# The last product of a feed-forward layer by seven block products instead of eight

## The chip, the cores and the metric

The kernel runs on one core of a Trainium2 chip. Its time is the device time of one execution in microseconds; the time before is the median of 3 executions. A profile of one further execution gives the span from the first to the last instruction, and the work of TensorE (PE; its weight loads are PEld), VectorE (DVE), ScalarE (ACT), GpSimd (POOL) and the DMA queues. SyncE (SP) only issues transfers.

## The reference

256 tokens of 1024 channels in float32 pass through two blocks: an mLSTM and a gated linear attention layer, each with a mixture of 16 experts behind it, and then an attention layer with a gated feed-forward layer. The change is in the very last part:

```python
def conv_ffn(y, w_up, conv_w, conv_b, w_down):
    u = y @ w_up
    ...
    gate, val = jnp.split(u, 2, axis=-1)
    return (jax.nn.silu(gate) * val) @ w_down
...
        y = rms_norm_2(h, ffn_norm[i])
        h = h + conv_ffn(y, w_up[i], conv_w[i], conv_b[i], w_down[i])
    return rms_norm_2(h, final_norm)
```

The last product is (256 tokens x 2816) @ (2816 x 1024). The result is added to the stream h, and each token is divided by its root mean square and multiplied by a gain row.

## The kernel before

All engines have instruction lists of their own, written out by hand, and meet by semaphores. Weights come through `weight_ring`, 9 slots of 128 x 4096 float32 in SBUF, in one order that SyncE's list fixes; a slot is loaded again when TensorE has counted `tile_used` for its last content, and `landed[slot]` tells TensorE of the arrival (`arrived`).

The feed-forward is `ffn()` of each engine. There are UPT = 11 tiles of w_up and N_DOWN = 6 tiles of w_down (numbers T_UP and T_DOWN on); a tile of w_down holds four blocks of 128 rows by 1024 columns, the last one two. FB = 22 such blocks are the 2816 rows.

- Up (L1172, in `up`): for each tile, 32 matmuls of a 128 x 128 block of weights on the 256 turned tokens `xT`, into banks 0 to 5 by turns. ScalarE takes the banks with the middle tap of the convolution (L1499, `taps`), VectorE adds the two other taps (L1966, `convolve`), ScalarE applies SiLU (L1508), and VectorE multiplies gate and value (L1977) into `ffh`, 22 blocks of 128 channels x 256 tokens in `phase_room`; each of the 11 multiplications makes two blocks and counts `ff_ready`.
- Down (L1206): for each tile of w_down, for both halves `tt` of the tokens, for its blocks `k` and both halves `j` of the 1024 columns, one matmul with 128 tokens of `ffh` as the stationary operand and 512 columns of the tile as the moving one:

```python
mm(PS[4 + 2 * tt + j][:, :], ffh[:, k, tt * P:(tt + 1) * P],
   w[:, k - 4 * i, j * 512:(j + 1) * 512], start=(k == 0), stop=(k == FB - 1))
```

  So 22 x 2 x 2 = 88 matmuls go to four banks (4 to 7), one for each quarter of the output. The last tile is ordered so that the quarters end one after the other (`out_rows`, `last_half`, `tile_used`).
- The end, `final_norm` on VectorE: `add` (L1985) adds a bank to a quarter of the stream `x_tok`; ScalarE squares it and sums along the row (L1515); `total` (L1990) adds the two halves' sums; ScalarE takes the root (L1523, `final_deviation`); VectorE takes the reciprocal (L2005, L2012) and `scale` (L1995) writes the finished quarter to `acc`, from where SyncE sends it out (L544). Of the three waiting steps the scale of the first quarter runs while ScalarE squares the last one.

Of the kernel before, what the change touches and what calls it, by code (L numbers as in the profile page):

```python
# [17 lines left out]
ALU = mybir.AluOpType  # L18
ACT = mybir.ActivationFunctionType
# [114 lines left out]
def build_in(nc, t, out, ctx):  # L134
    def sem(name):
        return ctx.enter_context(nc.semaphore(name))
# [135 lines left out]

    PS = [ctx.enter_context(nc.psum_tensor(f"bank{i}", [P, 512], F32)) for i in range(8)]
# [97 lines left out]
    last_half = sem("last_half")  # L371
    final_sum, final_square, final_total = sem("final_sum"), sem("final_square"), sem("final_total")
    final_root, final_rows = sem("final_root"), sem("final_rows")
# [15 lines left out]
    def arrived(pe, n):  # L389

        pe.wait_ge(landed[SLOT_OF[n]], landings(n))
# [278 lines left out]
    def _(pe):  # L670
# [490 lines left out]
        def ffn():  # L1161
# [31 lines left out]

            pe.wait_ge(conv_done, (UPT - 3) // 3 * 3 + 3)
            for i in range(N_DOWN):
                n = T_DOWN + i
                pe.wait_ge(ff_ready, min(2 * i + 2, UPT))
                arrived(pe, n)
                w = slot(n).rearrange("p (k n) -> p k n", k=4)
                ks = range(4 * i, min(4 * i + 4, FB))  # L1200
                for tt in range(TT):

                    by_half = i == N_DOWN - 1 and tt == 1
                    for k, j in ([(k, j) for j in range(2) for k in ks] if by_half
                                 else [(k, j) for k in ks for j in range(2)]):
                        last = mm(PS[4 + 2 * tt + j][:, :], ffh[:, k, tt * P:(tt + 1) * P],  # L1206
                                  w[:, k - 4 * i, j * 512:(j + 1) * 512], start=(k == 0), stop=(k == FB - 1))
                        if by_half and (k, j) == (FB - 1, 0):
                            last.then_inc(last_half, 1)
                    if i == N_DOWN - 1 and tt == 0:  # L1210
                        last.then_inc(out_rows, 1)
                last.then_inc(tile_used, 1)
# [14 lines left out]
    def _(act):  # L1227
# [257 lines left out]
        def ffn():  # L1485
# [25 lines left out]
            for tt in range(TT):  # L1511
                for j in range(2):
                    c = slice(512 * j, 512 * (j + 1))
                    act.wait_ge(final_sum, 2 * tt + j + 1)
                    f(acc[:, tt, c], x_tok[:, tt, c], ACT.Square, accum_out=half_squares[:, 2 * tt + j:2 * tt + j + 1]  # L1515
                      ).then_inc(final_square, 1)
                if tt == 0:
                    final_deviation(0)
# [19 lines left out]
    def _(dve):  # L1538
# [415 lines left out]
        def ffn():  # L1954
# [24 lines left out]
            final_norm(T_DOWN + N_DOWN - 1)  # L1979

        def final_norm(n):

            def add(tt, j):
                c = slice(512 * j, 512 * (j + 1))
                v.tensor_tensor(x_tok[:, tt, c], x_tok[:, tt, c], PS[4 + 2 * tt + j][:, :], ALU.add  # L1985
                                ).then_inc(final_sum, 1)
# [59 lines left out]
```

## Time and profile before

| | us |
|---|---|
| median of 3 executions | 1592.81 (1592.26 to 1593.27) |
| the profiled execution | 1592.34 |
| its span, first to last instruction | 1590.5 |
| TensorE busy | 1309.8 (82%) |
| VectorE busy | 303.6 (19%) |
| ScalarE busy | 215.1 (14%) |

The page gives busy times over the whole span, then the span in 40 slices of 39.8 us, in which a digit is the busy share in tenths. The chain of waits is followed back from the last instruction to whatever released it, step by step. The record of a matmul is longer than the distance to the next one, since matmuls overlap; a float32 matmul of the program is two records. A group's line has its count, busy time, mean length of one and the idle time before.

### The profile page before, as it was taken

Reading aid. Unit: us, or ns where it says so; the run is one execution under the profiler, and the core shown is the slowest. Engines: PE = TensorE matmul, PEld = TensorE weight load, DVE = VectorE, ACT = ScalarE, POOL = GpSimd, SP = SyncE. Lnnn points to the kernel's source line nnn. Section 1 sums busy time; section 2 is a strip of 40 time slices with the busy share of each in tenths; the row PEclk is TensorE's granted clock in tenths of the full one; section 3 lists DMA queues with packets and bytes.
Section 4 is the critical chain, followed back from the end, with each engine's and each line's share of the span. In section 5 each row is a group of like instructions: output and inputs, shape, how many; then the busy total and the mean of one; then the engine's idle time right before and its main releaser. Section 6 shows DMA issues by size and latency. Waiting matters only on the chain.

```text
span 1590.5 us, 19235 instructions
## 1 busy us (share of the span) xinstructions
PE 1309.8 (82%) x8543; PEld 733.8 (46%) x8543; DVE 303.6 (19%) x747; ACT 215.1 (14%) x446; POOL 88.5 (6%) x106
## 2 busy tenths in 40 slices
PE   9999978568667679999886667667679999999998
PEld 7454533223223235655533223223235854988843
DVE  1153301001001002554310000001003032222201
ACT  1132100000000001441200000000001033211100
POOL 0001000000000001450000000000001022000000
PEclk9999998888888899999998988988889999999999
DMA  9917799999999999625799999999999941443000
GB/s 346 391 68 301 316 427 428 427 428 427 427 427 427 427 414 371 246 112 222 290 427 427 428 427 428 427 427 427 428 420 382 352 155 53 159 150 141 0 0 27
DMA packets 88258, 501.34 MB, mean 315 GB/s; under 512 B 8348, under 2 KB 31248, under 8 KB 63856
## 3 DMA queue, kind: packets, MB, share of 16 engines
q1 hardware_dynamic: 85152, 490.23, 75.9%
q0 software_dynamic: 3024, 9.89, 1.8%
q8 instruction: 68, 1.11, 0.3%
q14 instruction: 14, 0.11, 0.0%
HBM read 499.02 MB, written 1.07 MB: 314 GB/s over the span
## 4 chain that ended last, share of the span: by engine, by line
PE 52%; DMA 39%; DVE 4%; another core or an unknown queue 2%; ACT 1%; issue 1%; SPq 0%; POOL 0%; DVEq 0%; ACTq 0%
DMA phase_room<-in_moe_w_down 15%; PE bank L1172 10%; DMA weight_ring<-in_moe_w_down 9%; DMA weight_ring<-in_moe_w_gate 6%; PE bank L725 6%; DMA weight_ring<-in_moe_w_up 6%; PE bank L771 5%; PE bank L1028 5%; PE bank L1206 5%; PE bank L742 5%; PE bank L1080 3%; PE bank L1067 3%; PE bank L730 3%; DMA phase_room<-in_moe_w_gate 2%; PE bank L950 1%
## 5 line engine op out<-in xcount | busy, mean ns | idle before, releaser
L1028 PE MATMUL bank<-weight_ring,x_tok 128*32 128x256 f32 x3328 | 229.0, 424 | 123.9 <-DMA weight_ring<-in_moe_w_up 104.8
L1028 PEld LDWEIGHTS bank<-weight_ring,x_tok 128*32 128x32 f32 x3328 | 112.0, 119 | 235.7 <-issue 98.2
L1067 PE MATMUL bank<-weight_ring,xT 128*32 128x512 f32 x864 | 132.2, 745 | 85.9 <-DMA weight_ring<-in_moe_w_down 79.4
L1172 PE MATMUL bank<-xT,weight_ring 128*128 128x256 f32 (+1 forms) x768 | 153.1, 362 | 0.3 <-ACT xT L1237 0.3
L1172 PEld LDWEIGHTS bank<-xT,weight_ring 128*128 128x128 f32 x768 | 136.3, 191 | 16.8 <-issue 0.6
L1080 PE MATMUL bank<-x_tok,xT 128*128 128x512 f32 x256 | 124.5, 631 | 0.0
L1875 DVE TENSOR_TENSOR xT<-xT,bank 128x256 f32<-128x256 f32 x32 | 13.5, 421 | 477.2 <-PE bank L1028 477.2
L1067 PEld LDWEIGHTS bank<-weight_ring,xT 128*32 128x32 f32 x864 | 28.0, 122 | 164.0 <-issue 71.0
L725 PE MATMUL bank<-xT,weight_ring 128*128 128x256 f32 x448 | 97.6, 380 | 0.7 <-ACT phase_room L1268 0.7
L725 PEld LDWEIGHTS bank<-xT,weight_ring 128*128 128x128 f32 x448 | 85.2, 191 | 13.6 <-ACT phase_room L1268 1.5
L1080 PEld LDWEIGHTS bank<-x_tok,xT 128*128 128x128 f32 x256 | 49.2, 203 | 86.8 <-issue 86.8
L742 PE MATMUL bank<-weight_ring,xT 128*128 128x512 f32 x192 | 87.6, 596 | 1.8 <-DVE norm_rows L1787 0.8
L771 PE MATMUL bank<-weight_ring,xT 128*128 128x512 f32 x192 | 83.5, 594 | 1.7 <-ACT xT L1237 1.2
L1206 PE MATMUL bank<-weight_ring,phase_room 128*128 128x512 f32 x176 | 75.7, 593 | 0.0
L1028 PE MATMUL bank<-phase_room,x_tok 128*32 128x256 f32 x768 | 51.9, 419 | 21.9 <-DMA phase_room<-in_moe_w_up 16.9
L1880 DVE COPY x_tok<-bank 128x512 f32<-128x512 f32 x32 | 22.1, 692 | 245.2 <-PE bank L1067 245.2
L1966 DVE SCALAR_TENSOR_TENSOR phase_room<-bank,phase_room 128x255 f32<-128x255 f32 (+1 forms) x88 | 36.4, 476 | 110.5 <-ACT phase_room L1499 110.1
L771 PEld LDWEIGHTS bank<-weight_ring,xT 128*128 128x128 f32 x192 | 36.2, 190 | 45.8 <-issue 45.1
L1206 PEld LDWEIGHTS bank<-weight_ring,phase_room 128*128 128x128 f32 x176 | 33.5, 191 | 41.6 <-issue 41.5
L742 PEld LDWEIGHTS bank<-weight_ring,xT 128*128 128x128 f32 x192 | 34.8, 191 | 37.8 <-issue 36.0
L1433 ACT ACTIVATE xT<-bank 128x256 f32<-128x256 f32 x32 | 12.3, 383 | 286.9 <-PE bank L1051 286.9
L1435 ACT ACTIVATE x_tok<-bank 128x512 f32<-128x512 f32 x32 | 19.1, 597 | 217.4 <-PE bank L1067 217.4
(241 smaller groups left out, 1047.1 us busy)
## 6 DMA issues: line engine op xcount, KB each, us to landing
weight_ring<-in_moe_w_up SPq DMA_DIRECT2D x54, 2048.0 KB, 50.1
weight_ring<-in_moe_w_down SPq DMA_DIRECT2D x54, 2048.0 KB, 49.4
weight_ring<-in_moe_w_gate SPq DMA_DIRECT2D x50, 2048.0 KB, 49.5
phase_room<-in_moe_w_gate SPq DMA_DIRECT2D x14, 2048.0 KB, 49.0
weight_ring<-in_w_up SPq DMA_DIRECT2D x22, 1024.0 KB, 7.7
phase_room<-in_moe_w_up SPq DMA_DIRECT2D x10, 2048.0 KB, 49.9
phase_room<-in_moe_w_down SPq DMA_DIRECT2D x8, 2048.0 KB, 49.7
weight_ring<-in_gla_w_in SPq DMA_DIRECT2D x6, 2048.0 KB, 22.3
```

The costliest lines, as they stand in the source:

```text
L725: last = mm(PS[b0 + c // 2][:, (c % 2) * S:(c % 2 + 1) * S], w[:, k, c * P:(c + 1) * P], xT[:, k, :], start=(k == 0), stop=(k == KC - 1))
L730: last = mm(PS[b0 + tt][:, :], xT[:, k, tt * P:(tt + 1) * P], w[:, k, :], start=(k == 0), stop=(k == KC - 1))
L742: last = mm(bank[:, :], xT[:, k, tt * P:(tt + 1) * P], w[:, k, :], start=(k == 0), stop=(k == KC - 1), skip_group_check=True)
L771: last = mm(PS[4 + 2 * tt + j][:, :], xT[:, k, tt * P:(tt + 1) * P], w[:, k, :], start=(k == 0 and not scaled), stop=(k == KC - 1), skip_g ...
L1028: last = mm(bank[q * CAP:(q + 1) * CAP, 0:S], xinT[:, 4 * r + k, j * CAP:(j + 1) * CAP], w[:, k, q * S:(q + 1) * S], start=(r == 0 and k = ...
L1067: last = mm(PS[i][k * CAP:(k + 1) * CAP, :], hidT[:, 4 * r + k, :], w[:, k, i * 512:(i + 1) * 512], start=(r == 0), stop=(r == 1), skip_gr ...
L1080: last = mm(PS[4 + 2 * tt + i][:, :], selT[:, tt * P:(tt + 1) * P], exp_t[:, i * 512:(i + 1) * 512], start=False, stop=True, skip_group_ch ...
L1172: last = mm(PS[bank_pair + c // 2][:, at + tokens.start:at + tokens.stop], w[:, k, c * P:(c + 1) * P], xT[:, k, tokens], start=(k == 0), s ...
L1206: last = mm(PS[4 + 2 * tt + j][:, :], ffh[:, k, tt * P:(tt + 1) * P], w[:, k - 4 * i, j * 512:(j + 1) * 512], start=(k == 0), stop=(k == F ...
L1435: f(exp_t[:, 0:512], PS[0][:, :], ACT.Copy).then_inc(exp_act, 1)
L1880: v.tensor_copy(exp_t[:, 512:1024], PS[1][:, :]).then_inc(exp_dve, 1)
L1966: last = v.scalar_tensor_tensor(dst, u, conv_cols[:, 2 - back, n:n + 1], dst, ALU.mult, ALU.add)
```

## The change

The output is seen as 2 x 2 quarters: two halves of tokens by two halves of columns. The inner dimension is split too, into the 11 even and the 11 odd blocks of 128. Then the product is one of 2 x 2 block matrices, left A (tokens x inner) and right B (inner x columns), and Strassen's scheme in Winograd's form makes it by seven products of blocks instead of eight:

- sums on the left: S1 = A21 + A22, S2 = S1 - A11, S4 = A12 - S2, S3 = A11 - A21
- sums on the right: T1 = B12 - B11, T2 = B22 - T1, T3 = T2 - B11, T4 = T2 - B21
- products, numbered as in the code: P1 = A11 B11, P2 = A12 B21, P3 = S4 B22, P4 = A22 T4, P5 = S1 T1, P6 = S2 T2, P7 = S3 T3
- output: C11 = P1 + P2, C12 = P1 + P6 + P5 + P3, C22 = P1 + P6 + P7 + P5, C21 = P1 + P6 + P7 - P4

A product is 11 matmuls of 128 x 128 on 128 x 512 into one bank. They come in the order `STEPS` = 1, 2, 3, 6, 5, 7, 4. Products 6 and 7 go on adding to bank 6, in which product 1 lies. VectorE makes all sums. Those of left blocks go to room that is free by then (`xT`, `conv`, and the ring slot of the last tile of w_up). Those of right blocks are written over blocks of w_down in the ring: T1 over B12, T2 over B22, T3 over B11, T4 over B21, in six instructions each, one for each tile, and each overwrites a block after its last reader. Each product has six pieces, one for each tile of w_down; TensorE waits before a piece for the sum that it reads (`right_ready`), and counts `down_step` behind it. VectorE adds banks to the stream nine times in place of four, with a wait on its own last addition (`sums_taken`) ahead of each, and tells ScalarE of a finished quarter by a separate increment (`added`).

The diff, cut to its core:

```diff
+    left_sums = {1: xT_t[:, 0:PAIRS * P], 2: spare[:, 0:PAIRS * P], 3: conv_t[:, 0:PAIRS * P],
+                 4: spare[:, PAIRS * P:2 * PAIRS * P]}
+    def left_block(tt, odd):
+        return ffh[:, odd::2, tt * P:(tt + 1) * P]
+    def right_block(i, odd, half):
+        rows = min(4, FB - 4 * i)
+        w = ring[:, SLOT_OF[T_DOWN + i] * TILE:SLOT_OF[T_DOWN + i] * TILE + rows * D]
+        return w.rearrange("p (k n) -> p k n", k=rows)[:, odd::2, 512 * half:512 * (half + 1)]
...
+            def product(x, left, odd, half, bank, first=True):
+                made = {3: 4, 4: 2, 5: 1, 6: 2, 7: 3}
+                for i in range(N_DOWN):
+                    if x == 1:
+                        pe.wait_ge(ff_ready, min(2 * i + 2, UPT))
+                        arrived(pe, T_DOWN + i)
+                    elif x == 4:
+                        pe.wait_ge(right_ready[4], i + 1)
+                    elif x in (5, 6, 7):
+                        pe.wait_ge(right_ready[made[x]], i + 1)
+                    w = right_block(i, odd, half)
+                    for r in range(w.shape[1]):
+                        p = 2 * i + r
+                        last = mm(PS[bank][:, :], left[:, p], w[:, r], start=(first and p == 0), stop=(p == PAIRS - 1),
+                                  skip_group_check=True)
+                    last.then_inc(down_step, 1)
-            for i in range(N_DOWN):
...
-                last.then_inc(tile_used, 1)
+            product(1, left_block(0, 0), 0, 0, 6)
+            product(2, left_block(0, 1), 1, 0, 7)
+            pe.wait_ge(left_ready, 3)
+            product(3, left_sum(4), 1, 1, 4)
+            pe.wait_ge(sums_taken, 1)
+            product(6, left_sum(2), 1, 1, 6, first=False)
+            product(5, left_sum(1), 0, 1, 5)
+            pe.wait_ge(left_ready, 4)
+            pe.wait_ge(sums_taken, 4)
+            product(7, left_sum(3), 0, 0, 6, first=False)
+            product(4, left_block(1, 1), 1, 0, 7)
...
+            dve.wait_ge(ff_ready, UPT)
+            dve.wait_ge(tile_used, T_UP + UPT)
+            v.tensor_tensor(left_sum(1), left_block(1, 0), left_block(1, 1), ALU.add).then_inc(left_ready, 1)
+            dve.wait_ge(left_ready, 1)
+            v.tensor_tensor(left_sum(2), left_sum(1), left_block(0, 0), ALU.subtract).then_inc(left_ready, 1)
+            dve.wait_ge(left_ready, 2)
+            v.tensor_tensor(left_sum(4), left_block(0, 1), left_sum(2), ALU.subtract).then_inc(left_ready, 1)
+            v.tensor_tensor(left_sum(3), left_block(0, 0), left_block(1, 0), ALU.subtract).then_inc(left_ready, 1)
+            for i in range(N_DOWN):
+                arrived(dve, T_DOWN + i)
+                v.tensor_tensor(right_block(i, 0, 1), right_block(i, 0, 1), right_block(i, 0, 0), ALU.subtract
+                                ).then_inc(right_ready[1], 1)
...
-            dve.wait_ge(out_rows, 4)
-            add(0, 0)
-            add(0, 1)
-            dve.wait_ge(last_half, 1)
-            add(1, 0)
+            step(1)
+            add(0, 0, 6)
+            step(2)
+            add(0, 0, 7)
+            added()
+            for i in range(N_DOWN):
+                step(3, i)
+                dve.wait_ge(right_ready[1], i + 1)
+                v.tensor_tensor(right_block(i, 1, 1), right_block(i, 1, 1), right_block(i, 0, 1), ALU.subtract
+                                ).then_inc(right_ready[2], 1)
+            step(3)
+            add(0, 1, 4)
...
+            step(6)
+            add(0, 1, 6)
...
+            step(5)
+            add(0, 1, 5)
+            added()
+            add(1, 1, 5)
             total(0)
             dve.wait_ge(final_root, 1)
             link(v.reciprocal(inv_spread[:, 2:3], deviation[:, 2:3]))
-            dve.wait_ge(gain_landed, 64)
-            dve.wait_ge(tile_used, n + 1)
-            add(1, 1)
+            dve.wait_ge(gain_landed, 48)
             scale(0, 0)
+            scale(0, 1)
+            step(7)
+            add(1, 1, 6)
+            added()
+            add(1, 0, 6)
+            step(4)
+            add(1, 0, 7, ALU.subtract)
+            added()
             total(1)
             dve.wait_ge(final_root, 2)
             link(v.reciprocal(inv_spread[:, 3:4], deviation[:, 3:4]))
-            scale(0, 1)
             scale(1, 0)
             scale(1, 1)
```

The loops of T3 and T4 (left out) have the form of T2's, T4's without a wait. ScalarE squares the quarters in the new order.

Three places in the instruction lists. TensorE at the last product, before (a line has the operands by name, the shape of the output, the count, and in brackets the semaphores waited for):

```order
L1206 MATMUL bank<-weight_ring,phase_room 128x512 [waits landed4,ff_ready,conv_done]
L1206 MATMUL bank<-weight_ring,phase_room 128x512 x15
L1206 MATMUL bank<-weight_ring,phase_room 128x512 [waits landed5,ff_ready]
L1206 MATMUL bank<-weight_ring,phase_room 128x512 x15
L1206 MATMUL bank<-weight_ring,phase_room 128x512 [waits landed6,ff_ready]
L1206 MATMUL bank<-weight_ring,phase_room 128x512 x15
```

The same product in the change (now L1230, without the waits in the first fence), and, with its waits, the stretch from the end of product 1 into product 6:

```order
L1194 MATMUL bank<-xT,weight_ring 128x256 x320
L1230 MATMUL bank<-weight_ring,phase_room 128x512 x22
L1230 MATMUL bank<-weight_ring 128x512 x22
L1230 MATMUL bank<-weight_ring,xT 128x512 x11
L1230 MATMUL bank<-weight_ring,phase_room 128x512 x22
```

```order
L1230 MATMUL bank<-weight_ring,phase_room 128x512 [waits landed0,ff_ready]
L1230 MATMUL bank<-weight_ring,phase_room 128x512 x11
L1230 MATMUL bank<-weight_ring 128x512 [waits left_ready]
L1230 MATMUL bank<-weight_ring 128x512 x10
L1230 MATMUL bank<-weight_ring 128x512 [waits right_ready2,sums_taken]
L1230 MATMUL bank<-weight_ring 128x512
L1230 MATMUL bank<-weight_ring 128x512 [waits right_ready2]
```

There are 77 matmuls where 88 stood, and from product 6 on a wait ahead of each second one, where there was one for 16.

VectorE in the change, from the last gated pair (L2010) over the left sums (L2015 to L2020) and T1 (L2023) to T2 (L2065) and T3 (L2071); before, the additions of the final norm followed the gated pairs at once:

```order
L2010 TENSOR_TENSOR phase_room<-phase_room 128x512 [waits conv_done,ff_silu] x2
L2015 TENSOR_TENSOR xT<-phase_room 128x1408 [waits tile_used,ff_ready]
L2017 TENSOR_TENSOR weight_ring<-xT,phase_room 128x1408 [waits left_ready]
L2019 TENSOR_TENSOR weight_ring<-phase_room,weight_ring 128x1408 [waits left_ready]
L2020 TENSOR_TENSOR phase_room<-phase_room 128x1408
L2023 TENSOR_TENSOR weight_ring<-weight_ring 128x2x512 [waits landed4]
...
L2040 TENSOR_TENSOR x_tok<-x_tok,bank 128x512 [waits down_step]
L2040 TENSOR_TENSOR x_tok<-x_tok,bank 128x512 [waits sums_taken,down_step]
L2065 TENSOR_TENSOR weight_ring<-weight_ring 128x2x512 [waits sums_taken,right_ready1,down_step]
L2065 TENSOR_TENSOR weight_ring<-weight_ring 128x2x512 [waits right_ready1,down_step] x4
L2065 TENSOR_TENSOR weight_ring<-weight_ring 128x512 [waits right_ready1,down_step]
L2040 TENSOR_TENSOR x_tok<-x_tok,bank 128x512 [waits sums_taken,down_step]
```

VectorE gets 28 new sums in this stage, four of 1408 elements a partition, twenty of 1024 and four of 512, and five more additions of banks.

## Rows read from the trace of the kernel before

**Rows 1.** The page, engines and slices (40 equal slices of the span).
```profile
PE 1309.8 (82%) x8543; PEld 733.8 (46%) x8543; DVE 303.6 (19%) x747; ACT 215.1 (14%) x446; POOL 88.5 (6%) x106
...
PE   9999978568667679999886667667679999999998
...
PEclk9999998888888899999998988988889999999999
DMA  9917799999999999625799999999999941443000
```

**Rows 2.** The chain of waits from 1440 us on: start us, us, what.
```profile
1439.80 68.20 PE bank L1172 x316
1508.01 75.55 PE bank L1206 x176
```

**Rows 3.** Timeline of TensorE, its weight loads, and the page's group: start us, us, op.
```profile
1507.84 75.70 PE L1206 MATMUL bank<-weight_ring,phase_room 128*128 128x512 f32 x176
...
1508.27 0.19 PEld L1206 LDWEIGHTS bank<-weight_ring,phase_room 128*128 128x128 f32 x1 [0.24 <-issue]
...
1521.15 0.19 PEld L1206 LDWEIGHTS bank<-weight_ring,phase_room 128*128 128x128 f32 x1 [0.24 <-issue]
1521.58 0.19 PEld L1206 LDWEIGHTS bank<-weight_ring,phase_room 128*128 128x128 f32 x1 [0.24 <-issue]
1522.01 0.19 PEld L1206 LDWEIGHTS bank<-weight_ring,phase_room 128*128 128x128 f32 x1 [0.24 <-issue]
...
1582.52 0.19 PEld L1206 LDWEIGHTS bank<-weight_ring,phase_room 128*128 128x128 f32 x1 [0.24 <-issue]
...
L1206 PE MATMUL bank<-weight_ring,phase_room 128*128 128x512 f32 x176 | 75.7, 593 | 0.0
```

**Rows 4.** Stretches: engines' busy time (records), granted TensorE clock, DMA share, GB/s.
```profile
1440.00:1507.84 67.84, 67.84 (x316) 59.87 (x315) 19.52 (x45) 11.22 (x23) 0.00 (x0) 1.00 0.21 78
1507.84:1515.00 7.16, 7.16 (x18) 3.24 (x17) 4.59 (x10) 4.05 (x7) 0.00 (x0) 1.00 0.00 0
1515.00:1583.54 68.54, 68.54 (x160) 30.10 (x158) 2.21 (x5) 2.83 (x9) 0.00 (x0) 1.00 0.00 0
1583.54:1590.50 6.96, 0.00 (x0) 0.00 (x0) 3.75 (x7) 1.04 (x4) 0.00 (x0) 0.80 0.39 151
```

**Rows 5.** Timeline of VectorE around the product.
```profile
1513.26 1.48 DVE L1977 TENSOR_TENSOR phase_room<-phase_room 128x512 f32<-128x512 f32 x2
...
1583.68 0.69 DVE L1985 TENSOR_TENSOR x_tok<-x_tok,bank 128x512 f32<-128x512 f32 x1 [0.53 <-PE bank L1206]
...
1585.67 0.16 DVE L2012 RECIPROCAL small<-small 128x1 f32<-128x1 f32 x1 [0.36 <-ACT small L1523]
1585.87 2.08 DVE L1995 SCALAR_TENSOR_TENSOR acc<-x_tok,small,head_gain 128x512 f32<-128x512 f32 x3
```

**Rows 6.** SyncE's transfers of w_down, and their time to landing.
```profile
1397.53 69.43 SPq L468 DMA_DIRECT2D weight_ring<-in_w_down  x6
...
DMA to landing us min/median/max: 4.9/6.3/7.8
```

**Rows 7.** VectorE's groups by shape: count, busy us, mean ns, idle before.
```profile
L1875 DVE TENSOR_TENSOR xT<-xT,bank 128x256 f32<-128x256 f32 x32 | 13.5, 421 | 477.2 <-PE bank L1028 477.2
...
L1977 DVE TENSOR_TENSOR phase_room<-phase_room 128x512 f32<-128x512 f32 x11 | 7.5, 683 | 0.1
...
L1995 DVE SCALAR_TENSOR_TENSOR acc<-x_tok,small,head_gain 128x512 f32<-128x512 f32 x4 | 2.8, 745 | 0.0
...
L1985 DVE TENSOR_TENSOR x_tok<-x_tok,bank 128x512 f32<-128x512 f32 x4 | 2.7, 686 | 66.4 <-PE bank L1206 66.4
...
L1822 DVE SCALAR_TENSOR_TENSOR acc<-x_tok,small,head_gain 128x1024 f32<-128x1024 f32 x2 | 2.6, 1285 | 0.1
...
L1746 DVE SCALAR_TENSOR_TENSOR acc<-phase_room,acc 128x2048 f32<-128x2048 f32 x1 | 2.3, 2293 | 8.4 <-ACT acc L1377 8.4
```

**Rows 8.** Timeline of ScalarE at the end.
```profile
1584.40 0.63 ACT L1515 ACTIVATE acc<-x_tok 128x512 f32<-128x512 f32 x1 [0.83 <-DVE x_tok L1985]
```

More of the change, by code:

```diff
@@ L1192, in ffn @@
                 up(n, 2 * (i % 3), slice(0, S)).then_inc(tile_used, 1)
-            pe.wait_ge(conv_done, (UPT - 3) // 3 * 3 + 3)
-            for i in range(N_DOWN):
[L1196 to L1211, printed above, removed]
-                last.then_inc(tile_used, 1)
+            def product(x, left, odd, half, bank, first=True):
[14 more added lines that the diff above has]
+                    last.then_inc(down_step, 1)
@@ L1510, in ffn @@
             f(small[:, 250:251], ones[:, 0:1], ACT.Sqrt, bias=rms_eps)
[L1511 to L1517, printed above, removed]
+            for i, (tt, j) in enumerate(((0, 0), (0, 1), (1, 1), (1, 0))):
+                c = slice(512 * j, 512 * (j + 1))
+                act.wait_ge(final_sum, i + 1)
+                f(acc[:, tt, c], x_tok[:, tt, c], ACT.Square, accum_out=half_squares[:, 2 * tt + j:2 * tt + j + 1]
+                  ).then_inc(final_square, 1)
+                if i == 1:
                     final_deviation(0)
@@ L1978, in ffn, with final_norm, step, add @@
                                 ).then_inc(ff_ready, 1)
-            final_norm(T_DOWN + N_DOWN - 1)
-        def final_norm(n):
-            def add(tt, j):
-                c = slice(512 * j, 512 * (j + 1))
-                v.tensor_tensor(x_tok[:, tt, c], x_tok[:, tt, c], PS[4 + 2 * tt + j][:, :], ALU.add
-                                ).then_inc(final_sum, 1)
+            dve.wait_ge(ff_ready, UPT)
[10 more added lines that the diff above has]
+                                ).then_inc(right_ready[1], 1)
+            final_norm()
+        def final_norm():
+            def step(x, i=N_DOWN - 1):
+                dve.wait_ge(down_step, N_DOWN * STEPS.index(x) + i + 1)
+            taken = 0
+            def add(tt, j, bank, op=ALU.add):
+                nonlocal taken
+                c = slice(512 * j, 512 * (j + 1))
+                if taken:
+                    dve.wait_ge(sums_taken, taken)
+                taken += 1
+                v.tensor_tensor(x_tok[:, tt, c], x_tok[:, tt, c], PS[bank][:, :], op).then_inc(sums_taken, 1)
+            def added():
+                dve.wait_ge(sums_taken, taken)
+                dve.sem_inc(final_sum, 1)
             def total(tt):
@@ L1996, in scale @@
                                        ALU.mult, ALU.mult).then_inc(final_rows, 1)
-            dve.wait_ge(out_rows, 4)
-            add(0, 0)
-            add(0, 1)
-            dve.wait_ge(last_half, 1)
-            add(1, 0)
+            step(1)
[10 more added lines that the diff above has]
+            add(0, 1, 4)
+            for i in range(N_DOWN):
+                dve.wait_ge(right_ready[2], i + 1)
+                v.tensor_tensor(right_block(i, 0, 0), right_block(i, 1, 1), right_block(i, 0, 0), ALU.subtract
+                                ).then_inc(right_ready[3], 1)
+            step(6)
+            add(0, 1, 6)
+            for i in range(N_DOWN):
+                v.tensor_tensor(right_block(i, 1, 0), right_block(i, 1, 1), right_block(i, 1, 0), ALU.subtract
+                                ).then_inc(right_ready[4], 1)
+            step(5)
+            add(0, 1, 5)
+            added()
+            add(1, 1, 5)
             total(0)
```

9 lines of the change are left out of this document (8 added, 1 removed).

## The prediction

> **What bounds the kernel now.** The page first: TensorE is busy for 82% of the span, VectorE for 19%, and the last slices, in which the changed code lies, read 9 for TensorE, 0 for DMA in most of them and 9 for its clock [rows 1]. Shares of a whole span do not price an edit in one stage, so the chain of waits is read next, from 1440 us on: 68.2 us of the up-projection (L1172), then 75.55 us of the down-projection (L1206), then about 7 us of small steps [rows 2]. Nothing but TensorE stands in the chain until 1583.56. That is the thing to see: each matmul pass taken out of L1206 shortens the run, as long as nothing new is waited for.
>
> Then the timeline of TensorE. The 88 products of the program are 176 MATMUL records (a float32 product is two passes), in one unbroken run from 1507.84 over 75.70 us [rows 3]. The record's mean of 593 ns is a length that overlaps the next one, so I price by the distance of starts instead: weight loads start at 1508.27 and at 1582.52, 173 steps apart, 0.4292 us each [rows 3]. The granted clock is 1.00, the 2.4 GHz level, in both stretches of the product and in the up-projection ahead of it [rows 4]. VectorE has 2.21 us of work in the 68.5 us from 1515 on [rows 4]: it is free, and the question is only whether its new work is ready in time.
>
> **The products.** Seven products of 11 are 77 matmuls in place of 88, all of the same shape (the order shows 77 of 128x512). 22 passes x 0.4292 = **9.44 us less**. One product takes 22 passes, also 9.44 us. If TensorE starts at 1507.84 as before and never waits, product 1 ends at 1517.3, 2 at 1526.7, 3 at 1536.2, 6 at 1545.6, 5 at 1555.1, 7 at 1564.5, 4 at 1573.9.
>
> The start is unchanged, since nothing ahead of it is touched. What product 1 now needs sooner: it goes through all 22 feed-forward blocks in 9.4 us, where the old loop took 75. Its fifth piece (four pieces x two matmuls x 0.858 later, 1514.7) needs the tenth gated pair, its sixth (1516.4) the eleventh. VectorE finishes these at about 1513.95 and 1514.74 [rows 5]. That is 0.8 and 1.7 us early, so no wait, but it is the tightest place of the whole change. The weights it needs are all there: the last w_down transfer is issued at 1397.53 + 69.43 = 1466.96 and lands at most 7.8 us later [rows 6].
>
> **The sums on VectorE.** No row has 128x1408 or 128x2x512. The nearest two-tensor rows: 256 elements 421 ns, 512 from SBUF alone 683, with a PSUM operand 686; the three-operand form takes 1285 at 1024 and 2293 at 2048 [rows 7]. The step from 256 to 512 is 1.02 ns an element, so 1024 elements take 0.683 + 512 x 1.02 = 1.21 us and 1408 take 1.60; the three-operand rows give 1.29 and 1.66 as the upper end. I take 1.21 and 1.60, because the rows with the same operation and both operands in SBUF are nearest. Four left sums: 6.4 us. One pass over the weights: 5 x 1.21 + 0.68 = 6.7 us, and there are four. With nine additions of product banks where there were four (5 x 0.686), VectorE gets 6.4 + 26.9 + 3.4 = 36.7 us more.
>
> Now their due times, in VectorE's order from 1514.74 on. The left sums end at 1516.4, 1518.1, 1519.7 and 1521.3. Product 3 needs the third at 1526.7: **7 us to spare**. First pass over weights (T1) until 1528.0; two additions of products 1 and 2, both done, until 1529.4. The second pass (T2) overwrites what product 3 reads, piece by piece behind it: its first piece ends at 1530.7, and product 6 wants it at 1536.2: **5.5 us to spare**, the smallest margin against VectorE's speed. Its last piece must wait for the end of product 3, ends at 1537.2 and is read at 1544.7. T3 ends at 1544.7, the addition of bank 6 behind product 6 at 1546.3, and product 7 waits for both until 1555.1: 8.7 us. T4 ends at 1553.0 for product 4 at 1564.5. The additions behind products 5 and 7, the root and both scales of the first 128 tokens lie under products 7 and 4. So I cost the sums at nothing; their cover is TensorE's own run, and without it a late piece would cost what it is late.
>
> **Waits and signals on TensorE.** It stops at 42 piece ends in place of 6, with one signal at each. In the weight loads the starts go on at 0.43 across the old piece border, where a wait and a signal stand (1521.15, 1521.58, 1522.01), and over all 173 steps with five borders the mean is 0.4292 [rows 3]. So a border costs nothing that I can see: taken as 0, upper end 0.03 us each. The Trainium skill ("TensorE: Matmul & The Clock Gate", The cost: per-tile semaphore tail) has 26.3 ns for each increment by a matmul, since they serialize. By that the 34 added signals would cost 0.9 us; the trace disagrees as far as it shows five borders, with matmuls of 0.43 us in between.
>
> **The tail.** From the end of TensorE to the end of the span it is 6.96 us (1583.54 to 1590.5). On it lie one addition, square, total, root, reciprocal, then three scales in 2.08 us [rows 5, 8]. In the change two scales are left there, the other two having moved under product 7: one pitch less, and with 745 ns for one [rows 7] that is (2.08 - 0.745) / 2 = 0.67 us. Against that, ScalarE is now told by a separate increment after VectorE has waited for its own addition. VectorE's own wait costs 0.04 (reciprocal end 1585.83, scale start 1585.87) [rows 5]; with the increment I take 0.1, bounds 0.03 and 0.3. Tail: **0.57 us less**. The final output goes out by the same transfers in the same order. The gain-row wait falls from 64 to 48; the row is loaded before the feed-forward begins, so either passes at once.
>
> **Sum.** The profiled execution took 1592.34 us (span 1590.5 and 1.84 around it). 1592.34 - 9.44 - 0.57 = 1582.33. The median of the three runs lies 0.47 above the profiled one, so against it: **1582.8 us**. TensorE should end at 1574.1.
>
> **The rivals.**
> (a) *Piece borders cost.* 36 more borders x 0.03 us, about what a dependent step costs on VectorE, is 1.1 us: 1583.9. For: waits now come every 1.7 us, not every 6.9. Against: the even starts. By the skill's figure above it would be 1583.7.
> (b) *VectorE's sums are slower by half*, because of rows 8 KB apart, operands written over themselves, or TensorE reading beside them. The margin before product 6 is used up from a factor of about 1.4 on. At 1.5 T2's first piece ends at 1538.0 (1.8 us late), T3 and the addition behind it at 1557.8, and TensorE ends 2.8 us later than forecast: 1585.6. Against: the 683 and 421 ns rows lie on one straight line, and were taken while TensorE ran at full pace.
> (c) *The other side: the sums take twice as long.* Then T2's first piece is ready at 1545.1, product 6 stands for 8.9 us and is paced by T2 until 1557.0; product 5 until 1566.4; T3 and the addition hold product 7 until 1571.0; TensorE ends at 1590.1, 6.5 us later than now. 1592.81 + 6.5 - 0.6 = 1598.7. It decides from a factor of about 1.8. Nothing in the rows up to 2048 elements speaks for it: 2293 ns is 1.12 ns an element.
> (d) *TensorE slows while VectorE reads and writes SBUF beside it.* A pass longer by 14% would eat the whole 9.4 us. Against: from 1507.84 to 1515 VectorE is busy for 4.59 of 7.16 us, and the clock and the step of 0.43 are what they are later, when it is idle [rows 3, 4]. If passes got 3% longer in the 37 us that VectorE works, that is 1.1 us.
> (e) *The change does less than it says.* 77 matmuls could be split into more passes; but shapes and type are the old ones. Excluded by the order but for a small rest.
>
> **How the numbers follow.** Forecast 0.84, (a) 0.06, (b) 0.04, (c) 0.02, (d) and (e) 0.04. A measurement of this kernel can tell about 0.2%, 3.2 us, from no change. Forecast, (a), (b) and most of (d) lie over 3.2 us below 1592.81: faster 0.95; same 0.02; slower 0.03. The range: the forecast's own bounds are 1582.5 (tail at its best) to 1584.1 (every border at 0.03, tail at 0.3); spread between runs is 0.5 each way, and between builds I allow as much again; to take in part of (b) the upper end goes to 1585.2, the lower to 1581.4.
>
> **What would show it.** TensorE's last group: 154 records with step 0.429, unbroken, ending at 1574.1. Wrong if idle time appears ahead of product 3, 6 or 7 with VectorE as its releaser. VectorE: 24 sums of weights of 1.2 us and 0.68, four of 1.6, busy 340 us in all, first piece of T2 ended by 1531. Tail from TensorE's end 6.4 us, with two scales in it. If the run is near 1592 and TensorE ends at 1574, the tail was mis-read; if TensorE ends late without idle time, it is (a) or (d).

## The result, and the profile after

The change took 1580.04 us (median of 4 executions, 1578.42 to 1580.87), the kernel before 1592.61 beside it: a ratio of 0.9919, 95% interval 0.9902 to 0.9937. The forecast was 1582.8 with a range from 1581.4, so the direction was right and the gain was larger than the range allowed: 12.6 us where I had worked out 10.0.

The page of the change. Busy time of the engines, and the slices of TensorE, VectorE, the clock and DMA, as in [rows 1]:

```profile
span 1577.4 us, 19243 instructions
...
PE 1299.6 (82%) x8521; PEld 728.7 (46%) x8521; DVE 339.0 (21%) x780; ACT 215.2 (14%) x446; POOL 88.6 (6%) x106
...
PE   8999977667667679999887766666669999999998
...
DVE  1153211001001002454411001001003013222274
...
PEclk9999999889878889999998788888899999999999
DMA  9927799999999999626699999999999961444000
```

22 matmul records fewer, VectorE 35.4 us more (36.7 forecast). The last product (now L1230) in the timeline of TensorE, where [rows 3] had one group of 176; the columns are start, length, engine, line and operands:

```profile
1504.98 19.05 PE L1230 MATMUL bank<-weight_ring,phase_room 128*128 128x512 f32 x44
1523.86 19.05 PE L1230 MATMUL bank<-weight_ring 128*128 128x512 f32 x44
1542.74 9.61 PE L1230 MATMUL bank<-weight_ring,xT 128*128 128x512 f32 x22
1552.18 19.05 PE L1230 MATMUL bank<-weight_ring,phase_room 128*128 128x512 f32 x44
```

No idle time stands ahead of any of the four groups (products 1 and 2; 3 and 6; 5; 7 and 4). From first to last it is 1552.18 + 19.05 - 1504.98 = 66.25 us, where 66.26 was forecast (154 x 0.4292 and the end of the last). What was not forecast is the first number: the product starts at 1504.98, not at 1507.84.

VectorE in the same stretch, by its timeline:

```profile
1510.40 1.47 DVE L2010 TENSOR_TENSOR phase_room<-phase_room 128x512 f32<-128x512 f32 x2
1511.91 1.62 DVE L2015 TENSOR_TENSOR xT<-phase_room 128x1408 f32<-128x1408 f32 x1
1513.57 1.62 DVE L2017 TENSOR_TENSOR weight_ring<-xT,phase_room 128x1408 f32<-128x1408 f32 x1
...
1518.30 6.36 DVE L2023 TENSOR_TENSOR weight_ring<-weight_ring 128x1024 f32<-128x1024 f32 x6
1524.58 1.47 DVE L2040 TENSOR_TENSOR x_tok<-x_tok,bank 128x512 f32<-128x512 f32 x2
1526.27 2.46 DVE L2065 TENSOR_TENSOR weight_ring<-weight_ring 128x1024 f32<-128x1024 f32 x2 [0.21 <-DVE x_tok L2040]
...
1571.27 0.69 DVE L2040 TENSOR_TENSOR x_tok<-x_tok,bank 128x512 f32<-128x512 f32 x1 [7.92 <-PE bank L1230]
1572.81 0.16 DVE L2048 TENSOR_TENSOR small<-small 128x1 f32<-128x1 f32 x1 [0.85 <-ACT acc L1548]
...
1573.52 1.42 DVE L2053 SCALAR_TENSOR_TENSOR acc<-x_tok,small,head_gain 128x512 f32<-128x512 f32 x2
```

A left sum takes 1.62 us (1.60 taken), a pass over the weights 6.36 us for six sums (6.7 taken: sums in a row start closer together than they are long). T2's first piece ends at 1527.5, product 6 begins at 1504.98 + 3 x 9.44 = 1533.3, so 5.8 us were to spare (5.5 forecast). The tightest place of the prediction held too: the last two gated pairs (L2010) end at about 1511.1 and 1511.87, and product 1 reaches them at 1511.85 and 1513.56, 0.8 and 1.7 us later, as forecast.

The tail from TensorE's end to the end of the span is 6.19 us, against 6.92 before. (The page rounds a span to 0.1 us; with the rounded spans the tails would be 6.17 and 6.96. The tails below are taken from the unrounded ends in the traces.)

So of the 13.04 us between the spans of the two profiled executions, 9.45 are the product, 0.73 the tail, and **2.86 were gained ahead of the product, where no instruction differs.** The experiments had to say what that is, and whether the 10.2 us behind it are what I took them for.

### The profile page after: what moved, and what is told of

Read it like the earlier page. It is cut to its first block, busy times and chain, and to the rows that moved or that the text cites. A ratio compares the mean times of both kernels' runs of the same rounds, so it can differ in the third digit from the quotient of the medians.

```text
span 1577.4 us, 19243 instructions
## 1 busy us (share of the span) xinstructions
PE 1299.6 (82%) x8521; PEld 728.7 (46%) x8521; DVE 339.0 (21%) x780; ACT 215.2 (14%) x446; POOL 88.6 (6%) x106
## 4 chain that ended last, share of the span: by engine, by line
PE 54%; DMA 37%; DVE 4%; another core or an unknown queue 3%; ACT 1%; issue 1%; SPq 0%; POOL 0%; DVEq 0%; ACTq 0%
DMA weight_ring<-in_moe_w_down 21%; DMA phase_room<-in_moe_w_down 12%; PE bank L1194 10%; PE bank L747 6%; PE bank L1050 6%; PE bank L793 5%; PE bank L764 5%; PE bank L1102 4%; PE bank L1230 4%; PE bank L1089 4%; DMA weight_ring<-in_moe_w_up 3%; PE bank L752 3%; PE bank L1028 1%; PE bank L972 1%; PE bank L812 1%
## 5 line engine op out<-in xcount | busy, mean ns | idle before, releaser
L1050 PEld LDWEIGHTS bank<-phase_room,x_tok 128*32 128x32 f32 x768 | 26.2, 121 | 48.0 <-issue 21.7
L699 PE MATMUL bank<-consts 128*128 128x256 f32 (+1 forms) x194 | 45.9, 386 | 1.8 <-DVE xT L1910 1.8
```

The costliest lines, as they stand in the source:

```text
L699: mm(bank[:, 0:right.shape[-1]], left, right, start=True, stop=True, skip_group_check=True)
L1050: last = mm(bank[q * CAP:(q + 1) * CAP, 0:S], xinT[:, 4 * r + k, j * CAP:(j + 1) * CAP], w[:, k, q * S:(q + 1) * S], start=(r == 0 and k = ...
```

## The experiments

All were compared with the kernel before on the same chip. "Front" is the time up to the first matmul of the last product.

**1. Both kernels again.** `before_again` is the kernel before.

> The kernel before, unchanged, once more. In the profiled runs the last product began at 1507.84 us before and at 1504.98 in the change, though no instruction ahead of it differs. Theory 'scatter' (the time up to the product varies from execution to execution, by transfers and by the clock that is granted after pauses of TensorE): the product begins anywhere from 1505 to 1509 here, and the time is 1591 to 1594. Theory 'build' (the changed program is laid out otherwise and its front part is really 2.9 us faster): it begins at 1507.8 within 0.5, time 1592.6.

`after_again`, `after_third` and `after_fourth` are the change.

> The change, unchanged, once more. From the start of the last product to the end of TensorE 66.25 us, tail 6.2 us, by both theories. 'Scatter': the product begins anywhere from 1505 to 1509, and the median lies nearer to 1582 than to 1580. 'Build': it begins at 1505.0 within 0.5, median 1580.

> The change, unchanged, a third time. If a program keeps its own front part from one job to the next ('program'), the median is again 1579.6 to 1580.1; if the front is drawn anew with each execution ('scatter'), more executions bring the median up towards 1582.7.

> The change a fourth time. If its own front is really 2 us shorter, the median is below 1581.5 once more; if the 14 executions so far were a lucky draw, 1582 to 1583.

Measured: `before_again` 1593.28 us (1590.69 to 1596.78, 12 executions), front of the traced one 1507.06. The change: 1579.64 (5 executions, front 1504.58), 1580.87 (5, front 1507.39), 1582.08 (6, from 1578.43 to 1586.08, front 1505.94). In each trace the product takes 66.25 or 66.26 us and the tail 6.18 or 6.19. With the first four, the change has 20 executions with median 1580.7 and standard deviation 1.8; the kernel before, in all comparisons, 94 with median 1592.8 and 1.7. The first three of before, which lay within about 1 us of each other, were a poor sample: a single execution is good for 1.7 us, not for 0.5. 'Build', a front of the change fixed within 0.5 us, falls; 'scatter' holds for single executions, but does not bring the change's median to 1582.7: three of its four medians lie 1.8 us or more below that, the fourth 0.6. Against the kernel before on the same chip the four gains are 12.6, 13.4, 12.1 and 10.2 us; the last is just what product and tail give.

**2. The form without the saving.** `eight_blocks` has the change's code with eight products and no sums:

```diff
-            product(1, left_block(0, 0), 0, 0, 6)
-            product(2, left_block(0, 1), 1, 0, 7)
...
+            product(1, left_block(0, 0), 0, 0, 6, stop=False)
+            product(2, left_block(0, 1), 1, 0, 6, first=False)
+            product(2, left_block(0, 0), 0, 1, 7, stop=False)
+            product(2, left_block(0, 1), 1, 1, 7, first=False)
...
```

> The change's form (even and odd blocks, one bank for a product, a wait and a signal at each piece, 48 pieces, the new order of quarters and the new tail) with all eight block products and no sums on VectorE. If the seventh of the saving is the one product and the form costs nothing: 176 passes in 75.7 us, tail 6.2 us, 9.4 us slower than the change. Rival, that the form itself has a part in the gain or a cost: the product takes another time than 75.7. For the time up to the product: 'scatter' 1505 to 1509, 'build' 1505.0 if new code or semaphores as such move it.

Measured: 1592.15 us, ratio 0.9994 (0.9983 to 1.0004), front 1508.47. In its chain of waits:

```profile
1500.00 8.63 PE bank L1194 x40
1508.63 75.55 PE bank L1230 x176
1584.18 0.02 issue
1584.20 0.70 DVE x_tok L2027
```

75.55 us are those of [rows 2] to the digit: 48 pieces with a wait and a signal each cost nothing, and the form has no part in the gain but for the tail, here 6.18 us. Rival (a) of the prediction falls.

**3. VectorE's work beside the old product.** `before_with_sums` has 28 sums of the change's sizes beside the eight products:

```diff
+            dve.wait_ge(ff_ready, UPT)
+            sizes = [1408] * 4 + ([1024] * 5 + [512]) * 4
+            for i, n in enumerate(sizes):
...
+                v.tensor_tensor(gb_t[:, 0:n], ffh_t[:, 0:n], ffh_t[:, 0:n], ALU.add).then_inc(extra_done, 1)
             final_norm(T_DOWN + N_DOWN - 1)
```

> The kernel before with 28 sums of the sizes of the change's (4 of 1408, 20 of 1024, 4 of 512 elements) on VectorE beside its last product, written to free room. It tells whether VectorE's work costs TensorE anything, and whether it is what moves the front part. Theory 'free cover': the product stays at 75.70 us with a step of 0.429, time 1593.0 within 1. Rival 'contention': passes further apart, product longer than 76. On the front: in the three traced programs with seven products it was 2 to 3.3 us shorter than in the first one of before, in the three with eight between 0.8 shorter and 0.6 longer. If VectorE's longer list is what moves it, the time here is 1590.

`seven_no_sums` is the change without them; all 28 sums are left out, and products 3 to 7 read what lies there.

> The change with all 28 sums left out (the semaphores are counted up at once), so that products 3 to 7 run on what happens to lie in their operands. Its output is not the reference's. Product 66.25 us as in the change, if the sums really cost nothing. On the front: if the shorter list of TensorE is what moves it, the time is that of the change, 1579.7; if the longer list of VectorE is, 1582.8; if it is only scatter from program to program, anything from 1579 to 1584.

Measured: 1593.16 us (ratio 1.0001, 0.9993 to 1.0010) and 1580.29 us. VectorE and TensorE of `before_with_sums` by their timelines, then TensorE's last group of `seven_no_sums`:

```profile
1515.61 34.71 DVE L1985 TENSOR_TENSOR norm_rows<-phase_room 128x1408 f32<-128x1408 f32 x28
```

```profile
1508.68 75.70 PE L1207 MATMUL bank<-weight_ring,phase_room 128*128 128x512 f32 x176
```

```profile
1505.80 19.05 PE L1230 MATMUL bank<-weight_ring,phase_room 128*128 128x512 f32 x44
...
1553.01 19.05 PE L1230 MATMUL bank<-weight_ring,phase_room 128*128 128x512 f32 x44
```

34.7 us of sums beside TensorE leave its 75.70 us as they were, and the change without its sums has the 66.26 us that it has with them. The sums are free on both sides; contention (rival d) falls.

**4. The margin.** `sums_twice` puts a second sum of the same size ahead of each, `sums_half_more` one of 0.45 of the size:

```diff
+        def extra(n):
+            n = int(n * 1)
...
+            v.tensor_tensor(gb_t[:, 0:n], ffh_t[:, 0:n], ffh_t[:, 0:n], ALU.add).then_inc(extra_done, 1)
...
             for i in range(N_DOWN):
+                extra(1024 if i < N_DOWN - 1 else 512)
                 dve.wait_ge(right_ready[2], i + 1)
```

> The change with a second sum of the same size, into free room, ahead of each of the 28 sums on VectorE, so each takes twice as long. Theory 'due times' (TensorE waits for nothing but the sums' due times, with some 5.8 us to spare ahead of product 6): by the lengths measured in the change the first piece of T2 ends 13.6 us later, product 6 waits 7.8 us and ends 10 us late, product 7 is held by T3 and starts 13.7 us late, TensorE ends 13.7 us later than in the change, product 80.0 us from first to last in place of 66.25. Rival 'cover' (the margins are wider, or the sums slow TensorE rather than hold it): no idle time in the product, and matmul starts further apart than 0.43 us while VectorE works.

> The change with each of the 28 sums preceded by one of 0.45 of its size, so that VectorE's sums take about one and a half times as long. 'Due times': the first piece of T2 ends 6.3 us later than in the change and about 0.5 us too late for product 6, nothing else is late, product 66.8 us. 'Cover': 66.25. By the margin of my prediction (a factor of 1.4) there should be a small wait, by the same figures as the 1585.6 there a wait of 1.8 us; the measured pitches in the change say less.

Measured: 1594.71 us and 1583.41 us. TensorE of `sums_twice`, then of `sums_half_more`:

```profile
1505.85 19.05 PE L1231 MATMUL bank<-weight_ring,phase_room 128*128 128x512 f32 x44
1524.73 9.60 PE L1231 MATMUL bank<-weight_ring 128*128 128x512 f32 x22
1541.82 12.42 PE L1231 MATMUL bank<-weight_ring 128*128 128x512 f32 x22 [7.48 <-DVE weight_ring L2081]
1554.08 9.60 PE L1231 MATMUL bank<-weight_ring,xT 128*128 128x512 f32 x22
1565.82 19.12 PE L1231 MATMUL bank<-weight_ring,phase_room 128*128 128x512 f32 x44 [2.13 <-issue]
```

```profile
1527.35 9.61 PE L1231 MATMUL bank<-weight_ring 128*128 128x512 f32 x22
1537.38 9.68 PE L1231 MATMUL bank<-weight_ring 128*128 128x512 f32 x22 [0.43 <-DVE weight_ring L2081]
```

With sums twice as long TensorE stands for 7.48 us ahead of product 6 (7.8 expected), product 6 takes 12.42 us in place of 9.6 because T2's pieces pace it, and product 7 waits 2.13 us more: 79.09 us in all (80.0 expected). The view names no releaser for that last wait; the addition of bank 6 behind T3, which product 7 waits for, ends at 1565.72, 0.1 us before product 7 starts. With the smaller extra sums it is one wait of 0.43 us and 66.93 us (66.8 expected). The due times are right, and the change stays ahead until its sums take nearly twice as long.

**5. Inert edits.** If the front belongs to the form of the program, it must follow that form. `after_one_more_op` and `before_one_more_op` add a copy of one column under the product, `after_two_more_ops` a copy of two columns and an activation. `eight_less_one` is `eight_blocks` without A21 B11, so the quarter C21 lacks that product. `seven_and_one` is the change with one product more:

```diff
-    STEPS = (1, 2, 3, 6, 5, 7, 4)
+    STEPS = (1, 2, 3, 6, 5, 7, 8, 4)
...
+            product(4, left_block(1, 1), 1, 0, 0)
```

> The change with one more instruction on VectorE, a copy of one column, while TensorE is in product 4: nothing ahead of the product is touched and nothing waits for it. If the 2.9 us at the front belong to seven products as such, the median stays at 1579.8 within 0.7. If each program has a front of its own that such an edit redraws ('program'), it can come out anywhere from 1579.5 to 1583.5, and up to 3 us from the change's.

> The kernel before with the same one more instruction on VectorE beside its last product. If the eight-product form has a fixed front, 1593 within 0.7; by 'program' anywhere from 1590 to 1594.

> The change with a copy of two columns on VectorE and one more activation of one column on ScalarE, both under the product. If the change's front is shorter because of seven products, 1580.6 within 0.7; if it is a matter of the single program, 1580 to 1583.5; with the front of before 1582.7.

> eight_blocks with one of its eight products left out (A21 B11), so that the quarter C21 lacks it: 77 matmuls, no sums, output not the reference's. Product 66.25 and tail 6.17 us by every theory. With the front of before the median is 1592.9 - 9.45 - 0.8 = 1582.7. If a shorter execution or list of TensorE shortens the front, 1580.6 as the change; if the single program decides, anything from 1580 to 1583.5.

> The change with one more product of 11 matmuls, into a bank that nobody reads, between products 7 and 4: the change's code and sums with the length of eight products. Product 75.7 us. With the front of before 1592.1; if the change's code has the shorter front, 1590.0; if the short execution has it, 1592.1.

Measured: 1581.65, 1593.21, 1580.47, 1580.31 and 1590.87 us. Set against what before (1592.8) and each program's own product and tail give, the medians lie 1.0 below, 0.4 above, 2.2, 2.3 and 1.2 below. The change itself lies 2.6, 3.0, 1.8 and 0.5 below in its four comparisons, the programs of experiments 3 and 4 2.3 below, 0.1 above (`sums_half_more`) and 0.7 below (`sums_twice`) with seven products, and 0.3 above with eight. `eight_blocks` is 0.1 above; `short_tail` and `split_columns` (experiment 7) are 1.0 below and level.

By the standard deviation of 1.7 us the median of five executions is itself uncertain by about 0.9 us (an estimate), so the place of a single program says little, and neither a front for each program nor one for all seven-product programs is shown or excluded by them one by one. Taken together they do differ. The mean time less the program's own product and tail is 1509.0 us over the 68 executions of programs with seven products, and 1510.2 over the 139 of programs with eight: 1.1 us, with a standard error of 0.25. The number of products alone is not what divides them, since `seven_and_one`, the change's code with eight products, is as low (1509.1 over 12 executions). I have no mechanism for that difference, and it stays open.

**6. What the front is made of.** The start of the same matmul can be read in each of 18 traces. From the trace, the start of the matmul that stands at 180 us in before, the time between it and those at 600, 785 and 1205 us (first expert layer; the layer between; second expert layer), and from the first score matmul of the attention to the first of its output projection:

| trace | front | start | experts 1 | between | experts 2 | attention |
|---|---|---|---|---|---|---|
| before | 1507.84 | 180.23 | 419.98 | 185.00 | 419.92 | 29.74 |
| before_again | 1507.06 | 179.52 | 420.12 | 185.00 | 419.67 | 29.77 |
| before_one_more_op | 1506.66 | 178.72 | 420.44 | 185.00 | 420.12 | 29.41 |
| eight_blocks | 1508.47 | 180.47 | 420.47 | 184.99 | 420.08 | 29.48 |
| before_with_sums | 1508.68 | 180.43 | 420.32 | 186.71 | 419.81 | 28.44 |
| seven_and_one | 1506.87 | 179.05 | 419.55 | 186.72 | 420.03 | 28.55 |
| the change | 1504.98 | 180.53 | 419.29 | 185.01 | 418.76 | 28.42 |
| after_again | 1504.58 | 178.56 | 419.12 | 185.00 | 420.32 | 28.62 |
| after_third | 1507.39 | 180.05 | 420.17 | 185.01 | 419.99 | 29.18 |
| after_fourth | 1505.94 | 180.57 | 420.15 | 185.02 | 418.78 | 28.44 |
| sums_half_more | 1508.46 | 180.08 | 420.30 | 186.70 | 419.97 | 28.44 |
| sums_twice | 1505.85 | 180.86 | 419.00 | 185.00 | 419.59 | 28.43 |

All that is left of the front, two stretches of 90.1 and 182.9 us, is the same within 0.03 us in all 18 traces. Of the 2.86 us between before and the change, 1.32 are in the attention, 0.69 and 1.16 in the expert layers, and the start is 0.30 longer. The start varies most, from 178.6 to 181.2 us over the 18 traces (181.16 in `split_columns`, whose front is the longest); why, I did not find. The other parts take one of a few values, and the change itself shows both in the expert layers and in the attention.

The expert layers are paced by the transfers of their weights. The same two stretches in before and in the change (the last three columns are the granted clock, the DMA share and GB/s):

```profile
180.23:600.21 419.98, 299.08 (x2712) 127.64 (x2705) 38.68 (x88) 24.92 (x54) 4.00 (x7) 0.88 1.01 426
785.21:1205.14 419.93, 295.22 (x2704) 127.85 (x2701) 40.16 (x91) 24.33 (x53) 0.00 (x0) 0.89 1.01 426
```

```profile
180.53:599.82 419.29, 297.20 (x2713) 127.66 (x2706) 38.68 (x88) 24.93 (x54) 4.01 (x7) 0.89 1.01 426
784.83:1203.58 418.75, 298.45 (x2704) 128.37 (x2701) 40.15 (x91) 24.33 (x53) 0.00 (x0) 0.87 1.01 426
```

The DMA engines are busy throughout, at 425.4 to 425.8 GB/s in every trace. By the DMA records 178.76 and 178.71 MB move in them before, 178.45 and 178.20 MB in the change. At 425.6 GB/s the missing 0.31 and 0.51 MB are 0.7 and 1.2 us, the whole difference: more of the weights had been loaded ahead of the stretch (by the start of the first, 48.95 MB had moved in the change and 48.66 before). What lets the loading run further ahead in some executions I did not find.

The layer between takes 185.0 us, but 186.7 in four traces (the three of the table and `split_columns`). In these four, and in no other, the granted clock falls once in it, for 3.4 us at 602 to 605 us, and half of that is the 1.7 us.

For the attention the length can be read from the clock too. The windows of 32 us around it, in before, in the change and in `after_third` (columns as above):

```profile
1294.00:1326.00 32.00, 24.84 (x180) 15.71 (x180) 20.43 (x105) 22.14 (x82) 17.62 (x18) 0.89 0.30 100
```

```profile
1294.00:1326.00 32.00, 25.72 (x185) 15.94 (x182) 19.65 (x104) 20.98 (x81) 17.62 (x18) 0.95 0.30 99
```

```profile
1294.00:1326.00 32.00, 25.08 (x182) 15.59 (x181) 20.34 (x105) 22.14 (x82) 17.61 (x18) 0.89 0.31 100
```

The clock falls to its lower level (1.2 GHz) once at the start of the attention, after TensorE has waited for VectorE and GpSimd, and is back after about 7 us in the first and third and after about 3 in the second (the missing 0.11 and 0.05 of 32 us, doubled, since half the clock is left). Where it fell 4.7 to 5.9 us behind the first score matmul, in six of the 18 traces, the low stretch was the long one and the attention took 29.2 to 29.8 us; where it fell after 6.4 to 7.7 us, in twelve, 28.4 to 28.6. The same eight matmuls in the chain of waits of before and of the change:

```profile
1302.22 1.58 PE bank L1116 x8
```

```profile
1300.42 0.86 PE bank L1138 x8
```

That is 1.3 us of the 2.86. It is no property of the change: `before_with_sums` has the short form, `after_third` has not. Why the clock falls earlier in one execution than in another, these traces do not show.

**7. A shorter end.** In both runs here product 4 is cut into two halves of 256 columns. `short_tail` moves the last quarter's scale to ScalarE besides.

```diff
+            for part in range(2):
+                for i in range(N_DOWN):
...
+                        last = mm(PS[7 - 3 * part][:, 0:256], left[:, p], w[:, r, 256 * part:256 * (part + 1)],
...
+            f(acc[:, 1, 512:D], acc[:, 1, 512:D], ACT.Copy, scale=inv_spread[:, 3:4]).then_inc(act_rows, 1)
```

> The change with a shorter end: product 4 in two halves of 256 columns, each with a bank of its own, so that only 256 columns are added and squared behind the last matmul; and the quarter that is ready earlier is multiplied by the gain under product 4 and scaled by ScalarE beside VectorE's last scale. From the end of TensorE: addition 0.27 less, square 0.25 less, scale 0.67 less, so a tail of 5.0 in place of 6.17 us; the product 0.1 longer (44 passes of 0.2163 for 22 of 0.4292). 1.1 us less than the change, 1578.6, if the front is the change's. Rival: ScalarE's scale starts later or is longer than VectorE's and ends last, gain under 0.6.

> The change with product 4 in two halves of 256 columns, so that only 256 columns are added and squared behind the last matmul; both last scales stay on VectorE, since in short_tail the two last transfers, started together, took what the parallel scale had saved. Tail 0.51 shorter than the change's 6.17 us, product 0.06 longer, as in short_tail: 0.45 us less from the product's start to the end, 71.97 us in place of 72.42. The total depends on the program's front and may come out above or below the change's.

Measured: 1581.83 and 1582.21 us. In `short_tail` the two scales do run together, by VectorE's and ScalarE's timelines:

```profile
1574.98 0.75 DVE L2067 SCALAR_TENSOR_TENSOR acc<-x_tok,small,head_gain 128x512 f32<-128x512 f32 x1
```

```profile
1575.04 0.72 ACT L1566 ACTIVATE acc<-acc,small 128x512 f32<-128x512 f32 x1 [0.29 <-DVE small L2122]
```

They end at 1575.76, but the span ends at 1579.45, 3.7 us later; in the change it ends 2.5 us behind the last scale. By the traces' landing times the two last transfers of 256 KB, issued 0.38 us apart here, land 2.53 and 2.91 us after their issue; in the change, issued 0.67 us apart, they take 2.05 us each. That they hold each other up is the likely reason, but no run tests it. Tail 6.3 us, nothing gained. `split_columns`, with one scale behind the other, has product 66.31 and tail 5.69, 72.00 us where the change has 72.44: 0.44 less, where 0.45 was expected. Its traced front was 1509.71, the longest of all, and the median, beside 1580.87 for the change on the same chip, shows none of it. I found no version that is measurably faster than the change.

## Why the prediction was wrong, and where it was right

- **The products**: 9.44 us forecast, 9.45 measured. That the chain of waits named TensorE alone, and that starts are to be counted and not record lengths, was right. The granted clock stayed at 1.00.
- **The sums cost nothing**: right, with 5.8 us to spare where 5.5 were forecast, shown by `seven_no_sums` and `before_with_sums`.
- **Borders of pieces**: taken as 0, were 0 (`eight_blocks`). The figure of the Trainium skill ("TensorE: Matmul & The Clock Gate", The cost: per-tile semaphore tail) would have made 0.9 us of them. The page gives it for small tiles that share the array and each signal at their end; with matmuls of 0.43 us between the signals, `eight_blocks` shows nothing of it.
- **The tail**: 0.57 forecast, 0.73 measured. The scale was worth 0.66. The addition began 0.04 us behind TensorE's end, not 0.14, the new handing over cost 0.06 more than the old one where I took 0.1, and the end behind the last scale was 0.03 shorter.
- **Rivals b and c**: the order of events was right, the sizes too large. In my working TensorE ended 2.8 us later with sums half longer and 16.0 us later with sums twice as long (1590.1 against 1574.1); the runs had 0.7 and 12.8. The reason is the pitch: a pass over the weights takes 6.36 us, not 6.7.
- **The step that failed**: "The start is unchanged, since nothing ahead of it is touched", and with it the range's term "spread between runs is 0.5 each way". The instructions are unchanged, but their time is not: the front lay between 1504.6 and 1509.7 us in 18 traces. Of the 2.86, 1.3 us is the clock at the attention and 1.9 the expert layers, which had less left to load; the start took 0.3 back. Why the change's own median stays about 2 us below what its product and tail give (1580.7 over 20 executions, against 1582.6) is open; experiments that changed the number of products, the code and the length one by one did not tie it to any of them. With the standard deviation of 1.7 us a median of four is uncertain by about 0.9 us (an estimate): the range would have reached down to about 1580.9, still above the 1580.04 measured.
- **The stated lower bound** does not follow from its terms. "Tail at its best" (0.03 for the increment in place of 0.1) gives 1582.7, not 1582.5, and a range from about 1581.7; the measured value lies below either.

Taken with all executions the change is worth 12.1 us (1592.8 to 1580.7), of which 10.2 are its own by the traces.

## What to carry to other kernels

Seven block products for eight pay where TensorE is the only thing in the chain, VectorE lies idle beside it, the weights are already in SBUF, and the sums can be put in an order in which each has microseconds to spare: give each sum a due time from the matmul pitch, and count VectorE's own pitch in a row, not its lengths. A local gain is to be read as the time from the first to the last instruction of the changed stage; the total of a 1.6 ms kernel moves by more than 1 us for reasons ahead of it. And a spread taken from three executions is no spread.

## What the runs showed of the hardware

- The attention, a stage behind a pause of TensorE, has two lengths, by when the clock falls in it: 28.4 to 28.6 or 29.2 to 29.8 us. The Trainium skill ("TensorE: Matmul & The Clock Gate", What's actually happening) has the clock set by how busy TensorE has lately been, on a window that does not start with the kernel, so that the point of change varies. The traces agree that the point varies: in 18 of them the fall lies 4.7 to 7.7 us behind the same matmul. That such a window is the reason, no run here shows.
- Sums of 1024 elements in a row take 1.22 us each but start 1.13 us apart.
- 34.7 us of two-operand work of VectorE on SBUF did not lengthen the 176 matmul passes that read SBUF beside it: 75.70 us with it and without.
- In the expert layers the DMA engines move 425.4 to 425.8 GB/s in all 18 traces; their two lengths are two amounts of data left to move.
- Of two output transfers of 256 KB, issued 0.38 us apart, the last landed 2.91 us after its issue; issued 0.67 us apart, 2.05 us.
